# A sample delta rule with stacked single-pass outer products, and the output norm of the prompt columns dealt out over its rounds

## The chip, the core and the metric

The kernel runs on one core of a Trainium2 chip. The metric is the time on the device in microseconds (us) of the whole program, one launch. Five engines work side by side and meet only at semaphores: TensorE (PE in the profile, with PEld for its weight loads), VectorE (DVE), ScalarE (ACT), GpSimd (POOL) and SyncE (SP, which here only issues DMAs).

## What is computed

Two consecutive layers of a hybrid decoder for 256 prompt tokens and 8 sample tokens that share the weights: layer 0 is a recurrent branch beside differential attention and a dense SwiGLU; layer 1 is a gated delta rule (8 heads of 128 x 128) and a mixture of 8 experts. The change touches the delta rule's sample part and the norm of its output. For each sample b and head h the reference does one step:

```
v_new = beta * (v - exp(g) * (k . S))          # S is the 128 x 128 state of (b, h)
o     = exp(g) * (q . S) + (q . k) * v_new
S     = exp(g) * S + outer(k, v_new)            # the state is read from HBM and written back
...
o = rmsnorm(o, onorm_g) * silu(z)               # over the 128 values of each head, prompt and sample tokens alike
y = o @ w_out
```

## The kernel before

Activations lie transposed, channels on partitions and the T = 264 tokens (TP = 256 prompt columns, then TS = 8 sample columns) along the row. All float32 products of activations with weights are made in three single-pass parts: both operands are split into a float32r high part and a low rest (`h_hi`, `h_lo`, `weight_hi`, `weight_lo`), and high x high, high x low and low x high are summed in PSUM. The delta rule's own small products are plain float32 matmuls; each of them shows as two records.

Every engine has one written list of instructions in program order; nothing is scheduled. A named signal (`sig`, `at`) is a count on a semaphore, and an engine that waits for one holds back all that is behind it in its list.

After the chunked delta rule of the prompt (it ends with `S_pr`, L1552, and fills columns 0 to 255 of `oT`) comes the sample part, which is what the change rewrites. It goes through the HC = 8 heads in rounds. The states of a head (8 samples, 512 KB) lie in one of four slots of `s_ring`: heads 0 to 3 are loaded long before; the states of head h + 4 can be loaded by GpSimd's queue (L563, L744 to L746) only when those of head h have been written back by ScalarE's queue (L1138). In a round

- TensorE makes k . S and q . S of the next head (`state_products`, L2167: 8 samples, each one float32 weight load of a 128 x 128 state and 2 columns), transposes v_new and k of this head into 8 rows (`state_rows`, L2177, L2178), and makes the outer products of the head before (`state_outer`, L2186: k as an 8 x 128 weight, a block-diagonal 8 x 1024 `v_diag`, in two matmuls of 512 columns, in plain float32);
- VectorE makes v_new and o of the next head (`sample_out`, L1637 to L1642), copies the k rows and spreads v_new over the blocks of `v_diag` (`sample_outer_in`, L1650, L1651), and adds the outer products to the states (`sample_state`, L1658);
- ScalarE scales the states by exp(g) (L1132) and issues the write-back (L1138).

`v_diag` and the PSUM banks of the outer products (5, 6 and 0, 1) are double.

Behind the last round comes the output norm of all 264 columns, one engine after another: ScalarE squares (L1141), TensorE sums over each head (L2201), ScalarE takes the root (L1143), VectorE the reciprocal (L1681), TensorE spreads it over 128 partitions (L2208, 8 heads), VectorE applies it (L1684) and multiplies by the gate `zT` (L1689), ScalarE makes `h_hi` (L828) and VectorE `h_lo` (L834). TensorE then starts the projection `w_out_o` (lines L858, L862, L869), which waits for `on_hi`. Router, dispatch and the eight experts (L2287 to L2308) follow. SyncE begins to load the first expert's weights (L629) when the last states are written back, since these use the same ring.

## Time and profile before

| | us |
|---|---|
| three timed runs, median (lowest to highest) | 1877.57 (1874.33 to 1878.81) |
| the profiled execution: its own time | 1878.5 |
| the profiled execution: its span in the trace | 1876.8 |

The span runs from the first instruction to the last; 1.7 us lie around it. TensorE's matmul row is busy 1739.3 us of the span, VectorE 1357.2, ScalarE 1056.0. The granted clock is 0.928 of full speed on average. A row such as "PE bank L2186" names an engine, what it writes and the line of the kernel; a time in a chain or timeline row is counted from the start of the span.

### The profile page before, as it was taken

What the parts mean: (1) busy time and instruction counts of PE and PEld (TensorE: products, weight loads), DVE (VectorE), ACT (ScalarE), POOL (GpSimd) and SP (SyncE); (2) the same over time, 40 slices, a digit from 0 to 9 for tenths busy, and PEclk for the clock granted to TensorE, in tenths of its full rate; (3) what the DMA queues carried; (4) which work ended last, traced back from release to release, by engine and by line L of the source; (5) the groups of instructions that cost most, each with busy time, mean ns of one, the idle gap of its engine ahead of it and who ended that gap; (6) DMA issues with size and microseconds to landing.
All of it is one profiled execution on the core that took longest, in us unless ns stands there. A gap on an engine that the chain in (4) does not pass through costs nothing.

```text
span 1876.8 us, 25201 instructions
## 1 busy us (share of the span) xinstructions
PE 1739.3 (93%) x9621; PEld 1483.8 (79%) x9621; DVE 1357.2 (72%) x1519; ACT 1056.0 (56%) x1019; POOL 122.9 (7%) x149
## 2 busy tenths in 40 slices
PE   7957899999777989889999999999999999999997
PEld 7826799998766877477888888888888888888885
DVE  6673355445755783456889889888898898888986
ACT  5332344335552223236767777777677777776774
POOL 5021021003221000010000000000000000000000
PEclk9955799999987887589999999999999999999999
DMA  7542144544340001446999989989999899899893
GB/s 258 180 138 67 65 162 156 202 158 142 135 135 8 1 1 45 129 163 215 375 336 346 373 319 360 375 309 372 346 338 368 322 355 375 310 368 376 310 370 131
DMA packets 199099, 445.48 MB, mean 237 GB/s; under 512 B 9473, under 2 KB 20899, under 8 KB 198975
## 3 DMA queue, kind: packets, MB, share of 16 engines
q1 hardware_dynamic: 184698, 423.88, 62.6%
q0 software_dynamic: 3872, 12.85, 2.4%
q10 hardware_dynamic: 10448, 7.65, 1.4%
q8 instruction: 55, 0.90, 0.2%
q14 instruction: 26, 0.21, 0.0%
HBM read 437.28 MB, written 7.29 MB: 237 GB/s over the span
## 4 chain that ended last, share of the span: by engine, by line
PE 79%; DVE 9%; ACT 5%; PEld 2%; issue 2%; DMA 1%; POOL 1%; PEldq 0%; DVEq 0%; ACTq 0%; SPq 0%
PE bank L2308 16%; PE bank L2287 11%; PE bank L2288 11%; PE bank L2292 11%; PE bank L858 5%; PE bank L862 5%; PE bank L869 5%; PE bank L2258 2%; ACT weight_hi L505 1%; PE bank L2268 1%; PE bank L2186 1%; DVE weight_lo L508 1%; PE bank L2167 1%; POOL weight_lo L559 1%; PE bank L2111 1%
## 5 line engine op out<-in xcount | busy, mean ns | idle before, releaser
L508 DVE TENSOR_TENSOR weight_lo<-weight_ring,weight_hi 128x2048 fp32r<-128x2048 f32 (+1 forms) x352 | 797.0, 2273 | 258.4 <-ACT weight_hi L505 236.6
L505 ACT ACTIVATE weight_hi<-weight_ring 128x2048 fp32r<-128x2048 f32 (+1 forms) x358 | 680.0, 1903 | 335.6 <-PE bank L869 118.7
L2287 PE MATMUL bank<-weight_hi,h_lo 128*128 128x512 f32 x896 | 355.1, 396 | 4.2 <-DVE h_lo L1746 4.2
L2288 PE MATMUL bank<-weight_hi,h_hi 128*128 128x512 f32 x896 | 350.0, 391 | 0.0
L2292 PE MATMUL bank<-weight_lo,h_hi 128*128 128x512 f32 x896 | 239.9, 390 | 0.0
L2287 PEld LDWEIGHTS bank<-weight_hi,h_lo 128*128 128x128 f32 x896 | 168.8, 188 | 38.7 <-DVE h_lo L1746 4.5
L2292 PEld LDWEIGHTS bank<-weight_lo,h_hi 128*128 128x128 f32 x896 | 168.2, 188 | 35.2
L2288 PEld LDWEIGHTS bank<-weight_hi,h_hi 128*128 128x128 f32 x896 | 169.0, 189 | 33.6
L858 PE MATMUL bank<-n_hi,weight_hi 128*128 128x264 f32 x608 | 104.2, 294 | 23.3 <-ACT h_f L1072 7.9
L2308 PE MATMUL bank<-weight_hi,h_lo 128*128 128x512 f32 x448 | 120.6, 391 | 1.8 <-DVE h_lo L1751 1.8
L2308 PE MATMUL bank<-weight_lo,h_hi 128*128 128x512 f32 x448 | 119.8, 389 | 0.0
L2308 PE MATMUL bank<-weight_hi,h_hi 128*128 128x512 f32 x448 | 119.8, 389 | 0.0
L508 DVE TENSOR_TENSOR weight_lo<-work,weight_hi 128x2048 fp32r<-128x2048 f32 x48 | 109.8, 2288 | 12.6 <-ACT weight_hi L505 12.6
L858 PEld LDWEIGHTS bank<-n_hi,weight_hi 128*128 128x128 f32 x608 | 86.7, 194 | 27.6 <-issue 26.0
L505 ACT ACTIVATE weight_hi<-work 128x2048 fp32r<-128x2048 f32 x48 | 92.1, 1919 | 26.8 <-PE bank L2292 20.4
L862 PE MATMUL bank<-n_hi,weight_lo 128*128 128x264 f32 x608 | 101.5, 290 | 2.8 <-POOL weight_lo L559 2.8
L2308 PEld LDWEIGHTS bank<-weight_hi,h_lo 128*128 128x128 f32 x448 | 83.5, 188 | 18.9 <-DVE h_lo L1751 2.1
L2308 PEld LDWEIGHTS bank<-weight_hi,h_hi 128*128 128x128 f32 x448 | 84.1, 188 | 17.6
L2308 PEld LDWEIGHTS bank<-weight_lo,h_hi 128*128 128x128 f32 x448 | 84.1, 188 | 17.5
L858 PE MATMUL bank<-h_hi,weight_hi 128*128 128x264 f32 x464 | 87.9, 294 | 9.0 <-ACT h_hi L828 5.9
L862 PEld LDWEIGHTS bank<-n_hi,weight_lo 128*128 128x128 f32 x608 | 86.7, 194 | 3.2 <-POOL weight_lo L559 3.2
L862 PE MATMUL bank<-h_hi,weight_lo 128*128 128x264 f32 x464 | 85.9, 290 | 1.5 <-DVE weight_lo L508 1.5
(465 smaller groups left out, 2226.7 us busy)
## 6 DMA issues: line engine op xcount, KB each, us to landing
weight_ring<-in_moe_wg SPq DMA_DIRECT2D x104, 1024.0 KB, 7.2
weight_ring<-in_moe_wu SPq DMA_DIRECT2D x96, 1024.0 KB, 7.4
weight_ring<-in_moe_wd SPq DMA_DIRECT2D x88, 1024.0 KB, 6.6
work<-in_moe_wd SPq DMA_DIRECT2D x24, 1024.0 KB, 7.2
weight_ring<-in_w_in_o SPq DMA_DIRECT2D x8, 2048.0 KB, 8.8
work<-in_moe_wu SPq DMA_DIRECT2D x16, 1024.0 KB, 6.0
weight_ring<-in_ffn_wg SPq DMA_DIRECT2D x5, 2048.0 KB, 7.8
weight_ring<-in_ffn_wu SPq DMA_DIRECT2D x5, 2048.0 KB, 7.8
```

Of the source, the lines that this page charges most:

```text
L505: return SC.activation(whi[:, p % SPLIT, 0:size], src, ACT.Copy).then_inc(sig("hi_done"), 1)
L508: V.tensor_tensor(wlo[:, p % SPLIT, 0:size], src, whi[:, p % SPLIT, 0:size].bitcast(F32), ALU.subtract)\
L559: GP.tensor_tensor(wlo[:, p % SPLIT, 0:size], src, whi[:, p % SPLIT, 0:size].bitcast(F32), ALU.subtract)\
L858: PE.matmul(out, hi[:, jj, cols_], a_hi[:, j0 + j, :], start=first and j == 0, stop=False)
L862: PE.matmul(out, lo[:, jj, cols_], a_hi[:, j0 + part * half + jj, :], start=False, stop=False)
L869: last = PE.matmul(out, hi[:, jj, cols_], a_lo[:, j0 + j, :], start=False, stop=last_one and j == k - 1)
L2111: last = PE.matmul(bank[STREAM[u]][:, k * P:(k + 1) * P], Am[:, h, :], Tt[:, h, :], start=True, stop=True)
L2258: last = PE.matmul(bank[(7, 3)[r]][:, jj * CAP:(jj + 1) * CAP], h_tok[:, i, j * P:(j + 1) * P], sel[:, i, :], start=i == 0, stop=i == NTT - 1)
L2287: PE.matmul(out, hte_l[:, j, :], hi[:, jj, :], start=j == 0, stop=False)
L2288: PE.matmul(out, hte_h[:, j, :], hi[:, jj, :], start=False, stop=False)
L2292: last = PE.matmul(out, hte_h[:, j, :], lo[:, jj, :], start=False, stop=j == KD - 1)
L2308: last = PE.matmul(bank[5 + hf][:, :], lhs[:, c % 2, k, :], rhs[:, kk, hf * CHUNK_COLS:(hf + 1) * CHUNK_COLS], start=c == 0 and k == 0 and ...
```

## The change

It does three things, all between the end of the prompt's delta rule and the start of `w_out_o`.

1. The outer products. k and v_new are split into a float32r high part and a rest, and stacked as 24 rows: (k high, k low, k high) against (v high, v high, v low). The sum over 24 rows is the same three-part product as elsewhere, in one float32r pass of 512 columns instead of one float32 matmul. The k rows of all heads are transposed once ahead of the rounds (`k_three`, eight transposes, two ScalarE copies to `k_rows`); each round transposes only the 24 v rows. VectorE makes the v split in each round ahead of its signal (two short instructions more before `s_v`), and no longer copies k rows. `v_diag` and the outer products' banks are single instead of double, so `state_outer(h)` waits for `sample_state(h - 1)`, and `sample_outer_in(h)` for `state_outer(h - 1)`. Three small DMAs on GpSimd's queue make the 24-row selector `same_row`.
2. The norm of the 256 prompt columns is taken into the rounds: squares ahead of round 0 (ScalarE), head sums in round 0 (TensorE, behind `state_rows(0)`), root in round 1 (ScalarE), reciprocal in round 1 (VectorE, behind `sample_state(0)`), two heads' spreading and application in each of rounds 2 to 5, the gate multiplication on GpSimd (behind the loads of heads 5, 6 and 7), `h_hi` in two parts in rounds 6 and 7.
3. The norm of the 8 sample columns comes behind round 7 as one small group of its own (64 columns), with a matmul against `ones`; `sample_state(7)`, the last addition, is moved behind it. `w_out_o` waits for `on_sample_hi`.

```diff
--- before.py
+++ after.py
...
-        v_new_blocks = (inv.rearrange("p a b -> p (a b)")[:, 2 * T:2 * T + TS * P], work[:, B_0 + 4 * GRP:B_0 + 6 * GRP])
-        v_diag = [v.rearrange("p (b e) -> p b e", b=TS) for v in v_new_blocks]
...
-        k_row = [inv[0:TS, 1, k * P:(k + 1) * P] for k in range(2)]
+        R3 = 3 * TS
+        outer_in = n_lo2[:].rearrange("p a b -> p (a b)")
+        v_diag = outer_in[0:R3, HC * TS:HC * TS + TS * P].rearrange("p (b e) -> p b e", b=TS)
+        k_rows = outer_in[0:R3, HC * TS + TS * P:HC * TS + (TS + HC) * P].rearrange("p (h d) -> p h d", h=HC)
...
-        outer_banks = ((5, 6), (0, 1))
+        outer_banks = (5, 6)
...
@@ GpSimd
             gp.wait_ge(*at("tail_written", 32))
+            for k in range(3):
+                gp.dma_start(same_row[k * TS:(k + 1) * TS, :], ident[0:TS, 0:TS]).then_inc(sig("same_row_made"), 16)
             GP.memset(gt_mask, 1.0)
...
+            def gate_rows(heads_):
+                for h in heads_:
+                    gp.wait_ge(*at("on_applied", h + 1))
+                    GP.tensor_tensor(oT[:, h, 0:TP], oT[:, h, 0:TP], zT[:, h, 0:TP], ALU.mult).then_inc(sig("on_gated"), 1)
+
             for h in range(4, HC):
                 gp.wait_ge(*at(f"state{h % 4}_written", 16))
                 load_state(gp, h)
+                if h >= 5:
+                    gate_rows(range((h - 5) * 2, (h - 5) * 2 + 2))
+            gate_rows(range(6, HC))
@@ ScalarE
+            SC.activation(o_prompt_sq, oT[:, :, 0:TP], ACT.Square).then_inc(sig("on_sq"), 1)
             act_e.wait_ge(*at("s_gb", 1))
...
+            for g in range(2):
+                act_e.wait_ge(*at("s_kt", g + 1))
+                SC.activation(k_rows[:, halves[g], :], bank[(4, 7)[g]][0:R3, :].rearrange("p (h d) -> p h d", h=NG), ACT.Copy)\
+                  .then_inc(sig("s_krows"), 1)
...
             for h in range(HC + 1):
...
                     last.then_inc(sig("s_scaled"), 1)
+                if h == 1:
+                    act_e.wait_ge(*at("on_ss", 1))
+                    SC.activation(o_prompt_r, bank[0][0:HC, 0:TP], ACT.Sqrt, bias=eps_t[0:HC, :], scale=1.0 / DV).then_inc(sig("on_root"), 1)
+                if h == HC - 2:
+                    o_high(0)
+                if h == HC - 1:
+                    act_e.wait_ge(*at("s_o", HC))
+                    SC.activation(o_sample_sq, oT[:, :, TP:T], ACT.Square).then_inc(sig("on_sample_sq"), 1)
...
+                    o_high(1)
+                    act_e.wait_ge(*at("on_done", 1))
+                    SC.activation(h_hi[:, :, TP:T], oT[:, :, TP:T], ACT.Copy).then_inc(sig("on_sample_hi"), 1)
...
-            act_e.wait_ge(*at("s_o", HC))
-            SC.activation(inv, oT[:], ACT.Square).then_inc(sig("on_sq"), 1)
-            act_e.wait_ge(*at("on_ss", 1))
-            SC.activation(inv[0:HC, 0, :], bank[4][0:HC, 0:T], ACT.Sqrt, bias=eps_t[0:HC, :], scale=1.0 / DV).then_inc(sig("on_root"), 1)
-            high_parts(act_e, oT, "on_done", "on_hi")
@@ VectorE
+            link(V.tensor_copy(k_three[:, :, 0:TS].bitcast(F32R), kT[:, :, TP:T]))
+            V.tensor_copy(k_three[:, :, 2 * TS:R3].bitcast(F32R), kT[:, :, TP:T])
+            V.tensor_tensor(k_three[:, :, TS:2 * TS].bitcast(F32R), kT[:, :, TP:T], k_three[:, :, 0:TS], ALU.subtract)\
+             .then_inc(sig("s_k_three"), 1)
...
-                V.tensor_tensor(vn_t, qS, eg, ALU.mult).then_inc(sig("s_v"), 1)
+                if h >= 2:
+                    dve.wait_ge(*at("s_vt", h - 1))
+                v3 = v_three[:, h % 2, :]
+                link(V.tensor_copy(v3[:, 0:2 * TS].rearrange("p (k b) -> p k b", k=2).bitcast(F32R), vn.unsqueeze(1).broadcast_to([P, 2, TS])))
+                V.tensor_tensor(v3[:, 2 * TS:R3].bitcast(F32R), vn, v3[:, 0:TS], ALU.subtract).then_inc(sig("s_v"), 1)
+                V.tensor_tensor(vn_t, qS, eg, ALU.mult)
...
-                if h >= 2:
-                    dve.wait_ge(*at("s_outer", h - 1))
+                if h == 0:
+                    dve.wait_ge(*at("same_row_made", 48))
+                else:
+                    dve.wait_ge(*at("s_outer", h))
...
-                link(V.tensor_copy(k_row[h % 2], vt[0:TS, P:2 * P]))
-                V.tensor_tensor(v_diag[h % 2][0:TS], ident[0:TS, 0:TS].unsqueeze(2).broadcast_to([TS, TS, P]),
-                                vt[0:TS, 0:P].unsqueeze(1).broadcast_to([TS, TS, P]), ALU.mult).then_inc(sig("s_vd"), 1)
+                V.tensor_tensor(v_diag, same_row.unsqueeze(2).broadcast_to([R3, TS, P]),
+                                vt[0:R3, 0:P].unsqueeze(1).broadcast_to([R3, TS, P]), ALU.mult).then_inc(sig("s_vd"), 1)
...
+                if h == 1:
+                    dve.wait_ge(*at("on_root", 1))
+                    V.reciprocal(o_prompt_r, o_prompt_r).then_inc(sig("on_inv"), 1)
+                if 2 <= h <= 5:
+                    normed(2 * (h - 2))
+                    normed(2 * (h - 2) + 1)
...
@@ TensorE
+            pe.wait_ge(*at("s_k_three", 1))
+            for g in range(2):
+                for h in range(g * NG, (g + 1) * NG):
+                    last = PE.transpose(bank[(4, 7)[g]][0:R3, h % NG * P:(h % NG + 1) * P], k_three[:, h, :], ident[:])
+                last.then_inc(sig("s_kt"), 1)
...
-                PE.transpose(vt[0:TS, 0:P], vn_s[h % 2], ident[:])
-                PE.transpose(vt[0:TS, P:2 * P], kT[:, h, TP:T], ident[:]).then_inc(sig("s_vt"), 1)
+                PE.transpose(vt[0:R3, 0:P], v_three[:, h % 2, :], ident[:]).then_inc(sig("s_vt"), 1)
...
-                if h >= 2:
-                    pe.wait_ge(*at("s_state", h - 1))
+                if h:
+                    pe.wait_ge(*at("s_state", h))
                 for k in range(2):
                     n = TS // 2
-                    last = PE.matmul(bank[outer_banks[h % 2][k]][:, :], k_row[h % 2],
-                                     v_diag[h % 2][0:TS, k * n:(k + 1) * n, :].rearrange("p b e -> p (b e)"), start=True, stop=True)
+                    last = PE.matmul(bank[outer_banks[k]][:, :], k_rows[:, h, :],
+                                     v_diag[:, k * n:(k + 1) * n, :].rearrange("p b e -> p (b e)"), start=True, stop=True)
                 last.then_inc(sig("s_outer"), 1)
...
+                if h == 0:
+                    head_sums()
+                if 2 <= h <= 5:
+                    head_rows(2 * (h - 2))
+                    head_rows(2 * (h - 2) + 1)
...
-            pe.wait_ge(*at("on_hi", 2))
+            pe.wait_ge(*at("on_sample_hi", 1))
```

TensorE, from the last sums ahead of the rounds to the outer products of head 0; before (L2159 is the sum q . k, L2167 the state products, L2186 the outer products):

```order
L2159 MATMUL bank<-work,ones 128x64
L2167 MATMUL bank<-work,weight_ring 128x2 x16
L2177 MATMUL bank<-ident,sm 8x128
L2178 MATMUL bank<-ident,work 8x128
L2167 MATMUL bank<-work,weight_ring 128x2 x8
L2177 MATMUL bank<-ident,sm 8x128
L2178 MATMUL bank<-ident,work 8x128
L2186 MATMUL bank<-work 128x512 x2
L2167 MATMUL bank<-work,weight_ring 128x2 x8
```

and now (L2216, L2229 and L2249 are the same three; L2220 transposes the k rows, L2257 are the head sums, L2265 the spreading of the norm):

```order
L2216 MATMUL bank<-work,ones 128x64
L2220 MATMUL bank<-ident,work 24x128 x8
L2229 MATMUL bank<-work,weight_ring 128x2 x16
L2241 MATMUL bank<-ident,work 24x128
L2257 MATMUL bank<-work,sm 8x256 x8
L2229 MATMUL bank<-work,weight_ring 128x2 x8
L2241 MATMUL bank<-ident,work 24x128
L2249 MATMUL bank<-n_lo_odd 128x512 x2
L2229 MATMUL bank<-work,weight_ring 128x2 x8
L2241 MATMUL bank<-ident,work 24x128
L2249 MATMUL bank<-n_lo_odd 128x512 x2
L2265 MATMUL bank<-work,ident 128x256 x2
```

The k transposes stand in front of the first state products, the head sums between the row transposition of head 0 and the state products of head 2, and two spreading matmuls behind the outer products from round 2 on.

VectorE, from the additions of heads 5 to 7 to the start of `w_out_o` (seven short memsets stand between the first three rows and the copy); before:

```order
L1658 TENSOR_TENSOR weight_ring<-weight_ring,bank 128x512 x2
L1650 COPY work<-bank 8x128
L1651 TENSOR_TENSOR work<-ident,bank 8x1024
L1658 TENSOR_TENSOR weight_ring<-weight_ring,bank 128x512 x4
L1679 COPY work<-bank 128x128
L1681 RECIPROCAL work<-work 8x264
L1684 SCALAR_TENSOR_TENSOR hT<-hT,par,bank 128x264 x8
L1689 TENSOR_TENSOR hT<-hT,work 128x1056 x2
L834 TENSOR_TENSOR h_lo<-hT,h_hi 128x1056 x2
L508 TENSOR_TENSOR weight_lo<-weight_ring,weight_hi 128x2048
```

and now (L1695 fills `v_diag`, L1702 adds to the states, L1710 and L1737 make `h_lo`, L1732 to L1734 are the sample norm):

```order
L1695 TENSOR_TENSOR n_lo_odd<-small,bank 24x1024
L1702 TENSOR_TENSOR weight_ring<-weight_ring,bank 128x512 x2
L1695 TENSOR_TENSOR n_lo_odd<-small,bank 24x1024
L1702 TENSOR_TENSOR weight_ring<-weight_ring,bank 128x512 x2
L1710 TENSOR_TENSOR h_lo<-hT,h_hi 128x4x256
L1732 RECIPROCAL work<-work 128x64
L1733 SCALAR_TENSOR_TENSOR hT<-hT,par,work 128x8x8
L1734 TENSOR_TENSOR hT<-hT,work 128x8x8
L1710 TENSOR_TENSOR h_lo<-hT,h_hi 128x4x256
L1737 TENSOR_TENSOR h_lo<-hT,h_hi 128x8x8
L1702 TENSOR_TENSOR weight_ring<-weight_ring,bank 128x512 x2
L1740 COPY work<-bank 128x128
```

Of the norm only the 64 sample columns and the low parts are left at the end, ahead of the last addition.

GpSimd, from the last mask to the router's sums (L563 and L570 load the states of heads 4 to 7); before:

```order
L740 AFFINE_SELECT work<-work 128x8x8
L740 AFFINE_SELECT work<-work 128x4x16
L740 AFFINE_SELECT work<-work 128x2x32
L740 AFFINE_SELECT work<-work 128x64
L563 DMA weight_ring<-in_state_delta_s 128x8x128 x4
L752 TENSOR_TENSOR work<-work 128x264 x7
```

and now (L756 is the gate multiplication):

```order
L749 AFFINE_SELECT work<-work 128x64
L570 DMA weight_ring<-in_state_delta_s 128x8x128 x2
L756 TENSOR_TENSOR hT<-hT,work 128x256 x2
L570 DMA weight_ring<-in_state_delta_s 128x8x128
L756 TENSOR_TENSOR hT<-hT,work 128x256 x2
L570 DMA weight_ring<-in_state_delta_s 128x8x128
L756 TENSOR_TENSOR hT<-hT,work 128x256 x4
L769 TENSOR_TENSOR work<-work 128x264 x7
```

The loads of heads 6 and 7 now stand behind two gate multiplications each.

## Rows read from the trace of the kernel before

**Rows 1.** Windows by stage: window, length, busy us (instructions) of each engine, PEclk, DMA.

```profile
722.30:789.40 67.10, 61.98 (x182) 38.33 (x182) 28.95 (x81) 20.13 (x67) 3.56 (x4) 0.51 0.35 95
789.40:808.80 19.40, 10.45 (x33) 5.32 (x33) 10.49 (x21) 5.88 (x5) 0.00 (x0) 0.68 0.85 297
808.80:856.80 48.00, 42.87 (x327) 38.48 (x327) 21.22 (x59) 21.22 (x33) 6.73 (x7) 0.96 0.31 110
856.80:1876.80 1020.00, 1008.04 (x4712) 834.40 (x4712) 875.81 (x551) 729.26 (x497) 0.00 (x0) 1.00 0.92 337
```

**Rows 2.** The chain that ended last, in the rounds: start, length, what.

```profile
723.18 6.50 PE bank L2167 x32
...
729.92 0.21 PE bank L2178
...
733.78 3.72 PE bank L2186 x4
737.52 1.29 DVE weight_ring L1658 x2
738.84 3.22 DMA out_delta_s_sample<-weight_ring
...
742.35 4.85 DMA weight_ring<-in_state_delta_s
747.24 3.58 PE bank L2167 x16
...
780.89 7.13 PE bank L2186 x8
```

**Rows 3.** The same chain, from the last write-back to `w_out_o`.

```profile
789.78 1.97 ACT work L1141
791.80 5.29 PE bank L2201 x16
...
797.62 1.80 DVE work L1681
799.47 5.16 PE bank L2208 x16
...
805.18 2.44 DVE hT L1689 x2
...
808.78 1.25 PE bank L858 x4
```

**Rows 4.** Timeline of the rounds: VectorE's short products and its spreading of v_new.

```profile
726.41 0.17 DVE L1637 TENSOR_TENSOR sm<-bank,sm 128x8 f32<-128x8 f32 x1 [3.86 <-PE bank L2167]
...
742.30 1.21 DVE L1651 TENSOR_TENSOR work<-ident,bank 8x1024 f32<-8x1024 f32 x1
```

**Rows 5.** The chain at the experts' start: a float32r matmul of 512 columns, clock low.

```profile
857.64 0.43 PE bank L2288
```

**Rows 6.** Timeline of GpSimd: the masks, and the router's sums.

```profile
588.70 4.57 POOL L740 TENSOR_SCALAR_AFFINE_SELECT work<-work 128x64 f32<-128x64 f32 x14
...
824.91 4.01 POOL L752 TENSOR_TENSOR work<-work 128x264 f32<-128x264 f32 x3 [56.10 <-ACT work L1152]
...
835.75 0.74 POOL L752 TENSOR_TENSOR work<-work 128x264 f32<-128x264 f32 x1 [0.60 <-ACT work L1152]
```

**Rows 7.** Timeline of VectorE: the first instruction that needs the masks.

```profile
600.13 0.87 DVE L1566 TENSOR_SCALAR work<-work,sm 128x128 f32<-128x128 f32 x4 [2.87 <-ACT work L1087]
```

**Rows 8.** Windows: the granted clock (third number from the end) around the norm and `w_out_o`.

```profile
795.00:800.00 5.00, 2.61 (x12) 1.11 (x10) 1.79 (x1) 0.47 (x1) 0.00 (x0) 1.00 1.05 402
...
808.80:812.20 3.40, 3.40 (x16) 3.40 (x17) 1.22 (x2) 0.00 (x0) 0.00 (x0) 0.52 0.00 0
812.20:815.60 3.40, 3.40 (x30) 3.40 (x30) 0.00 (x0) 0.00 (x0) 0.00 (x0) 1.00 0.02 5
```

**Rows 9.** Timeline: SyncE's first expert load, and ScalarE's first split of its data.

```profile
792.64 0.92 SPq L629 DMA_DIRECT2D weight_ring<-in_moe_wg  x2
...
822.28 1.92 ACT L505 ACTIVATE weight_hi<-weight_ring 128x2048 fp32r<-128x2048 f32 x1 [3.94 <-PEq L873]
```

More of the change, by code:

```diff
@@ L103, in program @@
               ("norm2_hi", KD), ("norm2_sq", KD), ("norm2_root", 1), ("ealog", 1), ("beta", 1), ("g_absexp", 1),
[L104 to L105 removed]
+              ("l2_sq", 2), ("l2_root", 1), ("eG", 1), ("on_sq", 1), ("s_egb", 1), ("s_qks", 1), ("s_krows", 2),
+              ("on_root", 1), ("on_hi0", 1), ("on_sample_sq", 1), ("on_sample_root", 1), ("on_hi1", 1), ("on_sample_hi", 1), ("norm3_sq", KD), ("lg_row", 1), ("norm3_root", 1), ("htok", 6),
               ("xtok", 6), ("gate_exp", 1))
@@ L1658, in sample_state, with o_low, normed @@
                     last = V.tensor_tensor(s_ring[h % 4][:, k * n:(k + 1) * n, :], s_ring[h % 4][:, k * n:(k + 1) * n, :],
-                                           heads(outer_banks[h % 2][k]), ALU.add)
+                                           heads(outer_banks[k]), ALU.add)
                 last.then_inc(sig("s_state"), 1)
+            def o_low(r):
+                part = slice(r * HALF, (r + 1) * HALF)
+                dve.wait_ge(*at(f"on_hi{r}", 1))
+                V.tensor_tensor(h_lo[:, part, 0:TP], oT[:, part, 0:TP], h_hi[:, part, 0:TP].bitcast(F32), ALU.subtract).then_inc(sig(f"on_lo{r}"), 1)
+            def normed(h):
+                dve.wait_ge(*at("on_b", h + 1))
+                V.scalar_tensor_tensor(oT[:, h, 0:TP], oT[:, h, 0:TP], col("onorm_g"), bank[h % 2][:, 0:TP], ALU.mult, ALU.mult)\
+                 .then_inc(sig("on_applied"), 1)
             sample_out(0)
@@ L2196, in _ @@
                     state_outer(h - 1)
+                if h == 0:
[3 more added lines that the diff above has]
+                    head_rows(2 * (h - 2) + 1)
+            pe.wait_ge(*at("on_sample_sq", 1))
+            PE.matmul(bank[2][:, 0:HC * TS], ones[:], o_sample_sq.rearrange("p h b -> p (h b)"), start=True, stop=True)\
+              .then_inc(sig("on_sample_ss"), 1)
             state_outer(HC - 1)
             PE.matmul(bank[7][:, 0:P], ones[:], lt_mask[:], start=True, stop=True).then_inc(sig("iota_psum"), 1)
[L2199 to L2210 removed]
+            pe.wait_ge(*at("on_sample_hi", 1))
             def router_logits(tiles):
@@ L2216, in router_logits @@
                     PE.matmul(bank[3][0:NE + 1, 0:T], w_router[:, j, :], hT[:, j, :], start=j == 0, stop=False)
-            dense_pe(pe, "w_out_o", KD, "out_o_psum", "out_o_added", low=("on_lo", 2),
+            dense_pe(pe, "w_out_o", KD, "out_o_psum", "out_o_added", low=("on_sample_lo", 1),
+                     before=((5, "s_state", HC), (7, "iota", 1)),
                      between=lambda n: n and router_logits(range(HALF)))
```

67 lines of the change are left out of this document (39 added, 28 removed).

## The prediction

> **What bounds the kernel now.** First the windows by stage. The experts, 1020 us, keep TensorE busy for 1008 us at the full clock (its fourth line, [rows 1]); the change touches nothing there, so what is won before them is kept if their weights come in time. Of the 86.5 us that the change rewrites, the rounds take 67.1 and the norm behind them 19.4 [rows 1]. TensorE's 61.98 busy us in the rounds mislead: the chain of waits shows what orders them [rows 2]. TensorE makes state products (3.58 for a head at the low clock) and float32 outer products (3.72), VectorE adds (1.29), then the states are written back (738.84) and the next head's loaded into the same slot until TensorE can start on them at 747.24. So from one addition's end at 738.8 to the products 8.4 us pass in which no engine matters, and this stretch is on the chain twice (slots 0 and 3). The granted clock in the rounds is 0.51, so TensorE runs at 1.2 GHz. The norm is a chain of single engines, TensorE busy for 10.45 of 19.4 us [rows 1, 3]; nothing lies beside it.
>
> **The outer products.** A float32r matmul of 512 columns costs 0.43 at the low clock [rows 5]; two make 0.86, with the first weight load 0.95, against 3.72: 2.8 saved a head. The trace has none with 24 rows; if it cost what float32 does it would be 3.72 (upper bound), the lower bound is 0.86, and I take 0.95, since columns and type are the same as in rows 5. One of two row transpositions goes too (0.21, [rows 2]). VectorE's spreading has 1024 columns as before, 1.21 [rows 4], on 24 partitions instead of 8. Its split of v_new puts two short instructions in front of the signal, one product moves behind it: 0.2 us a round, the spacing of the 0.17 us ones [rows 4]; between nothing, where TensorE is behind anyway, and 0.4.
>
> **The entry is longer.** Three VectorE instructions and eight k transposes (0.21 each, 1.7 us) stand ahead of the first state products: 725.0 instead of 723.18, +1.8; bounds 0 and +3. The Square (1.97, [rows 3]) and the two copies of k rows on ScalarE end near 726.4, before its first scaling can start, so nothing. Then two heads' products, 7.15, one transposition 0.2, and the head sums. The old ones took 5.29 [rows 3] and now stand on the path of head 2: 5.2 taken, bounds 7.1 (low clock throughout: 7.13 / 8 = 0.89 for a float32 record of 512 columns [rows 2], half of it 16 times) and 3.6 (high throughout). Head 2's products then run 737.6 to 741.2, where they ended at 733.3 before: **+7.9 us at this point**.
>
> **The laps through the slots.** Behind head 2's products VectorE makes v_new and o (1.5), spreads (1.2) and adds (1.3): slot 0 is ready at 745.2, +6.4 against 738.8, since 3.72 is no longer in between. The root is taken by then, the reciprocal (1.75) comes behind the addition. Write and load 8.4 again [rows 2]: head 4's products 753.7 to 757.3. Then 4.0 us instead of the old 0.44 + 3.72 + 1.29 = 5.45 to the end of slot 2's addition, 761.3; load; head 6's products 769.8 to 773.3. TensorE then does transposition, outer products and two spreading matmuls (0.2 + 0.95 + 1.7) and is at 776.2, which is also when slot 3 has its states (addition 767.7 + 8.5); head 7's products end at 779.8. Before they ended at 776.2: **+3.6**. The spreading matmuls of rounds 2 to 4 and the norm's application (two a round, near 1 us on VectorE) fall into the load waits, which are 3 to 6 us long; without that cover they would cost 1.7 a round.
>
> **The end.** Single buffers make the last two heads strictly serial: v_new and o of head 7 to 781.3, spreading of head 6 to 782.5, addition 5 to 783.8, outer products 6 to 784.8, spreading 7 to 786.0, addition 6 to 787.3. Then low part of half the prompt columns 1.2, and the sample norm: reciprocal of 64 columns 0.45 (64/264 of the 1.80 of rows 3), two short products 0.5, high part 0.2: `w_out_o` starts at 789.8. My own walk of this kind gives 810.3 for the old order, where the trace has 808.78 [rows 3]; most of that excess is in the old norm, 0.3 in the rounds, so I take **789.5**. Gain 808.8 - 789.5 = **19.3 us**: the whole norm goes (19.4), the rounds' 3.6 more is given back by the shorter end. The last addition, 1.3, now runs beside `w_out_o`.
>
> **Other queues.** The three small DMAs delay GpSimd's masks by under 3 us; these end at 593.3 and are first needed at 600.1 [rows 6, 7]: nothing. The loads of heads 6 and 7 stand behind gate multiplications whose inputs are ready rounds before. The last write-back comes at 795.9 instead of 792.6 and the first expert piece is split 13.5 us behind the start of `w_out_o`, at 803 instead of 822.28 [rows 9]; the load's cover falls from 29.6 us to 7. If it is late, ScalarE waits first; TensorE needs the piece only when the experts start, 34.5 us after that split (856.8 - 822.3, [rows 1, 9]): nothing. The gate multiplication costs GpSimd 0.74 alone, but three took 4.01 [rows 6] while VectorE was subtracting from SBUF. This row is my bound: eight at up to 1.34, off the path, since the last is due only by 788.
>
> The Trainium skill, SBUF — State Buffer, section "Who interferes with whom", speaks against putting these multiplications into the rounds: a VectorE instruction with two SBUF inputs and a GpSimd one that reads SBUF exclude each other, and the second waits for the whole of the first. By that rule the 4.01 us is explained, and VectorE's short products could wait 0.7 us each in rounds 4 to 6; the sum would be 2 us higher, as the second rival has it from the rows.
>
> **The rivals.** (a) *The rounds go as walked*: 1878.5 - 19.3 = 1859.2 for the profiled execution; the median lay 0.9 below it, so 1858.3. (b) *Waits add up*: head sums wholly at the low clock (+1.9), GpSimd and VectorE holding one another up as in the 4.01 of rows 6, three times on the path (3 x 0.74 = 2.2), 0.1 more on each VectorE instruction of the chain (1.2), slower transfers with writes and loads overlapping (0.3 a leg, 1.2): up to +6, 1862 to 1867. For it: each happens singly in the rows. (c) *The clock rises in the rounds*: it went to 1.00 after 3 us of the old head sums [rows 8]. If they do the same at 735, half the sums and head 2's products gain 3, and with luck a later head too: 1851 to 1855. Against it: through eight heads of products it stayed low. (d) *The 24-row product costs what float32 does*: the walk with 3.72 starts `w_out_o` at 804.4, 1873, a gain of 5.4 that cannot be told from none. (e) *Slower: the clock stays low in* `w_out_o` *and what follows*. It began at 0.52 and stood at 1.00 in the next window [rows 8], and the 48 us stage held 42.9 us of matmuls at 0.96 [rows 1]. With TensorE doing less right before it, the rise could come later; each us later costs half a us, and if the rise never came in that stage, 40 us: 1880 to 1898. It turns into a loss once over 39 us of matmuls run low. (f) *The gain is given back to expert weights* that come late: the first split would have to come over 30 us late before it costs the first us; then 1862 to 1878.
>
> **Numbers.** (a) 0.63, (b) 0.18, (c) 0.11, (d) 0.03, (e) 0.03, (f) 0.02. The likeliest is (a), and I predict 1858.5. The range takes in (a) with 3 us on either side for the head sums and the entry, (b), and the upper part of (c): 1852 to 1866. About 0.3%, 5.6 us, is what a measurement can tell from no change. Faster by more: all of (a), (b), (c) and half of (f), 0.93; within: (d) and the rest of (f), 0.04; slower: (e), 0.03.
>
> **What would show it.** Right: outer products near 0.95 a head; head sums of about 5 us between the products of heads 1 and 2; first products at 725; TensorE still waiting for loads of heads 4 and 6; head 7's products ending near 780; `w_out_o` starting near 789.5, and 48 us from there to the experts. Wrong: outer rows of 0.9 us each; no load waits left (then VectorE or TensorE is the bound of a round); GpSimd's loads issued well after the write-back landed; ScalarE waiting for expert data near 803; a low clock past 795.

## The result, and the profile after

The changed kernel takes 1857.98 us (median of four runs, 1856.56 to 1862.84), the one before 1878.19 (1874.33 to 1879.15): a ratio of 0.9899, with a 95% interval of 0.9881 to 0.9917. The forecast was 1858.5. The profiled execution took 1856.56 us, with a span of 1854.9.

The windows by stage, with the columns of [rows 1]: rounds and sample norm, `w_out_o` to dispatch, experts.

```profile
722.30:788.50 66.20, 53.75 (x200) 39.70 (x200) 35.46 (x105) 27.09 (x77) 9.33 (x12) 0.53 0.32 88
788.50:836.60 48.10, 42.85 (x327) 38.46 (x327) 23.56 (x69) 21.19 (x33) 6.72 (x7) 0.96 0.69 241
836.60:1854.90 1018.30, 1006.73 (x4712) 833.50 (x4712) 875.46 (x552) 729.32 (x497) 0.00 (x0) 1.00 0.93 337
```

What took 86.5 us in two stages of [rows 1] is one stage of 66.2: its 20.3 us are the gain. The stage behind it is as long as before and its clock as high (48.1 and 0.96 against 48.0 and 0.96). The experts are 1.7 us shorter in this execution and 1.3 longer in another one below; the change has no part in that.

The chain that ended last, in the rounds (start, length, what), answers to [rows 2]:

```profile
723.38 1.58 PE bank L2220 x8
724.97 6.62 PE bank L2229 x32
...
731.82 6.20 PE bank L2257 x16
738.02 1.89 PE bank L2229 x16
...
742.32 1.28 DVE weight_ring L1702 x2
743.62 3.22 DMA out_delta_s_sample<-weight_ring
...
747.12 4.95 DMA weight_ring<-in_state_delta_s
...
752.12 3.57 PE bank L2229 x16
...
755.93 1.16 PE bank L2249 x2
...
758.32 1.28 DVE weight_ring L1702 x2
759.62 3.34 DMA out_delta_s_sample<-weight_ring
...
763.24 4.80 DMA weight_ring<-in_state_delta_s
...
768.08 3.57 PE bank L2229 x16
...
773.03 1.71 PE bank L2265 x4
774.74 3.56 PE bank L2229 x16
...
788.55 1.25 PE bank L875 x4
```

L2220 are the k transposes, L2229 the state products, L2257 the head sums, L1702 the additions, L2249 the outer products, L2265 the spreading matmuls, L875 the first group of `w_out_o`. The laps through slots 0 and 2 stand on the chain as forecast. TensorE's waits for the loads of the states, in total, times, longest; in the kernel before and in this one:

```profile
PE bank L2167 <- DMA weight_ring<-in_state_delta_s: 4.3, 2, 2.2
...
PE bank L2229 <- DMA weight_ring<-in_state_delta_s: 7.5, 2, 4.7
```

So the float32r products took work off TensorE, the norm's matmuls were put in, and what TensorE then still waited for loads is 7.5 us, where it was 4.3.

The profiles of this study are compared by one distance: from the prompt's last delta-rule step (720.06 in the kernel before, 720.26 in this one) to the first instruction of `w_out_o`. It is 88.7 us before and 68.3 after.

### The profile page after: what moved, and what is told of

It reads as the page before. It is cut to its first block, busy times and chain, and to the rows that moved or that the text cites. A ratio compares the mean times of both kernels' runs of the same rounds, so it can differ in the third digit from the quotient of the medians.

```text
span 1854.9 us, 25220 instructions
## 1 busy us (share of the span) xinstructions
PE 1719.8 (93%) x9607; PEld 1479.3 (80%) x9607; DVE 1354.8 (73%) x1532; ACT 1057.0 (57%) x1024; POOL 127.2 (7%) x160
## 4 chain that ended last, share of the span: by engine, by line
PE 79%; DVE 10%; ACT 4%; PEld 2%; issue 2%; DMA 1%; POOL 1%; PEldq 0%; DVEq 0%; ACTq 0%; SPq 0%
PE bank L2384 16%; PE bank L2363 11%; PE bank L2364 11%; PE bank L2368 11%; PE bank L875 5%; PE bank L879 5%; PE bank L886 5%; PE bank L2334 2%; ACT weight_hi L512 1%; PE bank L2344 1%; DVE weight_lo L515 1%; PE bank L2229 1%; POOL weight_lo L566 1%; PE bank L2168 1%; PEld bank L879 1%
## 5 line engine op out<-in xcount | busy, mean ns | idle before, releaser
L875 PE MATMUL bank<-n_hi,weight_hi 128*128 128x264 f32 x608 | 104.8, 295 | 22.9 <-ACT h_f L1089 7.9
L875 PEld LDWEIGHTS bank<-n_hi,weight_hi 128*128 128x128 f32 x608 | 87.0, 195 | 27.3 <-issue 26.0
L512 ACT ACTIVATE weight_hi<-work 128x2048 fp32r<-128x2048 f32 x48 | 92.1, 1919 | 26.8 <-PE bank L2368 20.4
L875 PE MATMUL bank<-h_hi,weight_hi 128*128 128x264 f32 x464 | 87.8, 294 | 5.3 <-DVE work L1314 1.7
```

The costliest lines, as they stand in the source:

```text
L512: return SC.activation(whi[:, p % SPLIT, 0:size], src, ACT.Copy).then_inc(sig("hi_done"), 1)
L875: PE.matmul(out, hi[:, jj, cols_], a_hi[:, j0 + j, :], start=first and j == 0, stop=False)
```

## The experiments

All kernels, one line each. The distance, the time from there to the experts' first matmul and the clock are of the profiled execution; the times and ratios are of all runs. Kernels of one set shared a chip and the runs of the kernel before, whose medians were 1879.2, 1878.4 and 1876.3 in sets 1 to 3.

| set | kernel | to `w_out_o` | to experts | mean clock | median (lowest to highest) | ratio to before (95%) |
|---|---|---|---|---|---|---|
| 0 | before | 88.7 | 48.1 | 0.928 | 1878.19 (1874.33 to 1879.15) | |
| 0 | changed | 68.3 | 48.1 | 0.932 | 1857.98 (1856.56 to 1862.84) | 0.9899 (0.9881 to 0.9917) |
| 1 | after_again | 70.0 | 48.9 | 0.930 | 1859.42 (1852.94 to 1861.37) | 0.9884 (0.9866 to 0.9903) |
| 1 | sums_late | 64.0 | 48.3 | 0.938 | 1857.08 (1849.79 to 1857.74) | 0.9885 (0.9868 to 0.9901) |
| 1 | tail_early | 63.7 | 49.9 | 0.930 | 1853.99 (1853.51 to 1856.03) | 0.9866 (0.9850 to 0.9883) |
| 1 | both | 58.8 | 50.4 | 0.937 | 1854.48 (1848.34 to 1856.04) | 0.9872 (0.9856 to 0.9889) |
| 2 | outer_only | 86.3 | 49.4 | 0.928 | 1876.15 (1868.49 to 1878.99) | 0.9988 (0.9977 to 0.9999) |
| 2 | outer_f32 | 82.3 | 47.9 | 0.927 | 1871.74 (1865.88 to 1873.34) | 0.9962 (0.9949 to 0.9976) |
| 2 | gate_dve | 67.9 | 48.1 | 0.931 | 1857.68 (1856.83 to 1860.02) | 0.9895 (0.9878 to 0.9911) |
| 2 | half_states | 64.6 | 48.2 | 0.931 | 1853.84 (1853.03 to 1856.10) | 0.9872 (0.9856 to 0.9889) |
| 3 | after_third | 64.8 | 47.9 | 0.937 | 1856.94 (1852.20 to 1858.50) | 0.9891 (0.9871 to 0.9910) |
| 3 | both_again | 62.6 | 50.4 | 0.931 | 1850.95 (1849.85 to 1854.60) | 0.9862 (0.9843 to 0.9881) |
| 3 | root_behind | 62.0 | 50.6 | 0.931 | 1851.31 (1848.96 to 1854.59) | 0.9858 (0.9837 to 0.9879) |
| 3 | rows_early | 60.2 | 49.9 | 0.931 | 1851.47 (1846.03 to 1854.23) | 0.9858 (0.9836 to 0.9880) |

### The changed kernel itself, twice more

> The changed kernel unchanged, so that the other kernels of this comparison have it beside them. Every theory: 1858 us as in its first timing (1856.6 to 1862.8), and in the trace outer products of 1.2 us a head, head sums of 6.2, the first instruction of w_out_o near 788.5.

> The changed kernel unchanged, beside the three below on one chip. Every theory: 1858 to 1860 us; where the mean granted clock of an execution is 0.938 instead of 0.931, about 6 us less, since in the earlier comparison the one such execution of it took 1852.9 and the others 1859.1 to 1861.4.

The medians lie within 1.5 us of the first, but the distance to `w_out_o` came out as 68.3, 70.0 and 64.8: 5 us between executions of one kernel. In after_again the path went through slot 1, whose write-back took 4.55 us and whose load 5.37. In after_third the clock differed. Its windows around the end of the delta rule:

```profile
600.00:720.00 120.00, 100.93 (x819) 97.38 (x818) 90.75 (x281) 32.32 (x77) 0.00 (x0) 0.91 0.01 1
715.00:720.00 5.00, 3.55 (x31) 3.20 (x30) 2.82 (x12) 1.30 (x2) 0.00 (x0) 1.00 0.04 11
720.00:725.00 5.00, 5.00 (x39) 4.93 (x37) 1.16 (x8) 4.88 (x14) 0.00 (x0) 0.77 0.33 97
```

and its chain:

```profile
720.66 4.65 PE bank L2229 x32
725.54 5.54 PE bank L2257 x16
```

The clock of the prompt's stage, which the change leaves alone, was 0.91 (0.88 in the first execution over 600 to 720), that stage ended 3.7 us earlier, and the clock fell later, so that two heads' products took 4.65 instead of 6.62 and the head sums 5.54 instead of 6.20. The three profiled executions with a mean clock of 0.937 or 0.938 (after_third, sums_late, both) all show 0.91 from 600 to 715 us and 4.65 or 4.66 for these products; the others that have the k transposes show 0.88 or 0.89 and 6.62. The one execution of after_again with a mean clock of 0.938 took 1852.9 beside 1859.1 to 1861.4. So a step of some 6 us between executions comes with the clock of a stage ahead of the change (why it differs, no run shows), and distances below are compared at like clocks.

### One part alone

outer_only: from the changed kernel, everything of the norm put back where it stood.

```
-                if h == 0:
-                    head_sums()
-                if 2 <= h <= 5:
-                    head_rows(2 * (h - 2))
-                    head_rows(2 * (h - 2) + 1)
...
+            pe.wait_ge(*at("on_sq", 1))
+            for i in range(HC):
+                last = PE.matmul(bank[4][0:HC, 0:T], pick[:, 2 * HC - 1 - i:3 * HC - 1 - i], inv[:, i, :],
...
```

> Part 1 of the change alone: stacked float32r outer products with their single buffers and the k transposes ahead of the rounds; the whole norm of 264 columns stands behind the rounds as in the kernel before. Theory (the time is won by taking the norm off the end; the outer products are on the chain only at the turns of two slots and behind the last heads): the rounds lose the 6.2 us of head sums that the changed kernel has in them, so that the last addition ends near 785.4, 4 us before the last write-back of the kernel before, the norm's chain of 19 us follows, and w_out_o starts near 804.5: a gain of 4 to 5 us, time 1873 to 1875. Rival (TensorE is the bound of the rounds, as its 61.98 busy us of 67.1 look, and 2.5 us less for each of 8 heads counts in full): w_out_o near 788, time 1858, and the norm's dealing out would be worth nothing.

A gain of 2.4 us at `w_out_o`, and 2.2 in the medians, by the interval of the ratio hardly to be told from none: the rival, by which TensorE is the bound, falls, and the theory's gain of 4 to 5 was not reached either. The rounds did what the theory said and more: TensorE waited 13.5 us for loads, where it was 4.3,

```profile
PE bank L2195 <- DMA weight_ring<-in_state_delta_s: 13.5, 4, 6.2
```

and the last addition ends 63.5 us behind the delta rule's last step, where it was 69.3, 5.7 earlier. But then the norm took 22.8 us instead of 19.5. Its chain (L2231 are the head sums, L2238 the spreading, L867 `w_out_o`), to be read beside [rows 3]:

```profile
783.53 6.35 PE bank L2231 x16
...
792.25 7.42 PE bank L2238 x16
...
803.82 1.25 PE bank L867 x4
```

and the windows:

```profile
790.00:795.00 5.00, 2.75 (x6) 2.16 (x7) 2.77 (x3) 0.37 (x1) 0.00 (x0) 0.73 1.05 387
795.00:800.00 5.00, 4.66 (x11) 2.99 (x9) 2.75 (x6) 0.00 (x0) 0.00 (x0) 0.50 0.95 350
...
805.00:810.00 5.00, 5.00 (x27) 5.00 (x26) 0.05 (x1) 0.00 (x0) 0.00 (x0) 0.57 0.00 0
```

The same matmuls that took 5.29 and 5.16 took 6.35 and 7.42, because the clock, 1.00 behind the old head sums [rows 8], was down at 0.50 during most of the spreading and 0.57 into `w_out_o`, whose stage is 1.4 us longer. Ahead of the norm TensorE now had two float32r products (1.20 each) with waits between them, where it had 7.13 us of float32 products without a gap [rows 2]. So 3.3 + 1.4 of the 5.7 us went to a lower clock. That less work ahead is the cause of the late rise fits, and was not tried by itself.

outer_f32: the other way round, the float32r pass taken back.

```
-                    last = PE.matmul(bank[outer_banks[k]][:, :], k_rows[:, h, :],
-                                     v_diag[:, k * n:(k + 1) * n, :].rearrange("p b e -> p (b e)"), start=True, stop=True)
+                    last = PE.matmul(bank[outer_banks[k]][:, :], k_rows[:, h, :].bitcast(F32),
+                                     v_diag[:, k * n:(k + 1) * n, :].rearrange("p b e -> p (b e)").bitcast(F32), start=True, stop=True)
```

> The changed kernel with one thing undone: the 24-row outer products are plain float32 matmuls, on the same rows and buffers. It measures the disputed price (24 rows in float32 against 24 rows in float32r) and what it is worth. Theory: 3.7 to 3.9 us a head instead of 1.2; since the single buffers put them in series with spreading and addition, they count at slot 0's turn, at slot 2's turn, in the rounds of heads 5 to 7 and in the end: w_out_o 15 us later, near 804, time 1873. Rival (TensorE's time in the rounds is hidden behind the loads except at the two turns): 2.6 us twice, w_out_o near 794, time 1863.

14.0 us at `w_out_o` (theory 15), 1871.7 us (theory 1873). The chain in the middle of the rounds:

```profile
756.41 3.70 PE bank L2249 x4
760.11 1.71 PE bank L2265 x4
761.82 3.50 PE bank L2229 x16
765.55 3.71 PE bank L2249 x4
769.26 1.71 PE bank L2265 x4
```

A 24-row float32 product takes 3.70 us, the old 8-row one 3.72 [rows 2]: the 16 further rows cost nothing that these rows show. No DMA stands between these rows. TensorE waited only once for a load, 1.8 us, where the changed kernel waits 7.5, so here it is the bound.

Together the two kernels say what the parts are worth. Both have the single buffers, whose own price was not measured. Stacked products alone give 2.4 us, the dealt-out norm with float32 products 6.5 (88.7 - 82.3), both 20.4. Given the other, each is worth 14 to 18: the norm needs TensorE time and free banks in the rounds, and the short products make the time. The norm dealt out over the old double buffers was not tried, since it uses banks 0 and 1, which these held.

### The lap of a slot

half_states:

```
-            gp.dma_start(s_ring[h % 4], A["state_delta_s"][0, :, h].rearrange("b d e -> d b e")).then_inc(sig(f"state{h % 4}_loaded"), 16)
+            gp.dma_start(s_ring[h % 4][:, 0:TS if h < 4 else TS // 2], A["state_delta_s"][0, 0:TS if h < 4 else TS // 2, h].rearrange("b d e -> d b e")).then_inc(sig(f"state{h % 4}_loaded"), 16)
...
-                q.dma_start(O["delta_s_sample"][0, :, h].rearrange("b d e -> d b e"), s_ring[h % 4]).then_inc(sig(f"state{h % 4}_written"), 16)
+                q.dma_start(O["delta_s_sample"][0, 0:TS // 2, h].rearrange("b d e -> d b e"), s_ring[h % 4][:, 0:TS // 2]).then_inc(sig(f"state{h % 4}_written"), 16)
```

> It leaves out samples 4 to 7 of the loads of heads 4 to 7 and of all write-backs of the states: every transfer of the rounds carries half the bytes, all computation stays. Theory (the rounds' pace is the lap write-back, issue, load of 8.4 us through slots 0 and 2): a leg shrinks by less than half, since part of it is fixed; the lap comes down to about 6.5, heads 4 and 6 have their states 1.9 us earlier each, w_out_o near 785, time about 1854. Rival 1 (the engines set the pace, the loads are hidden): w_out_o at 788.5. Rival 2 (the lap is all bytes): 4.2 us a lap, then TensorE and VectorE become the bound near 782.

Slot 0's lap in its chain:

```profile
741.84 2.32 DMA out_delta_s_sample<-weight_ring
744.44 3.60 DMA weight_ring<-in_state_delta_s
```

From addition to products 6.3 us instead of 8.5 (743.60 to 752.12 in the changed kernel), TensorE's waits for loads 3.7 instead of 7.5, `w_out_o` 3.7 earlier (theory 3.5), 1853.8 us (theory 1854; gate_dve, in the same set and within 0.4 us of the changed kernel at `w_out_o`, took 1857.7). Head 6's products began 4.8 us earlier, but head 7's then waited 1.1 us for the load of slot 3, so not all of it reached the end. Half the bytes took 72% of the write's time and 73% of the load's. If a leg is a fixed part and one that goes with the bytes, the fixed part is 1.4 us of the write's 3.22 and 2.25 of the load's 4.95 (an estimate from these rows): a little under half. Both rivals fall.

### GpSimd beside VectorE

gate_dve:

```
-                if h >= 5:
-                    gate_rows(range((h - 5) * 2, (h - 5) * 2 + 2))
-            gate_rows(range(6, HC))
...
+                dve.wait_ge(*at("on_applied", h + 1))
+                V.tensor_tensor(oT[:, h, 0:TP], oT[:, h, 0:TP], zT[:, h, 0:TP], ALU.mult).then_inc(sig("on_gated"), 1)
```

> The gate multiplication of the norm (eight of 256 columns) is made by VectorE right behind each application of the norm instead of by GpSimd. Theory: VectorE waits for TensorE in rounds 2 to 5 anyway, so 2 x 0.4 us more a round are hidden; the two short VectorE instructions that took 0.60 and 0.48 instead of 0.17 while GpSimd issued a load or multiplied come down, if GpSimd's multiplication was the reason for the second (0.48) and the issue of a load for the first (0.60, which then stays): w_out_o within 1 us of 788.5, time 1857 to 1859. Rival 1 (the two engines hold one another up on the path by more than those two rows show): 2 us faster. Rival 2 (VectorE's rounds 4 and 5 are full): 1.5 us slower.

The rows in question, in the timeline of the changed kernel:

```profile
763.24 0.92 POOL L570 DMA_DIRECT2D weight_ring<-in_state_delta_s  x1 [7.21 <-DMA out_delta_s_sample<-weight_ring]
...
763.48 0.60 DVE L1685 TENSOR_TENSOR hT<-work,sm 128x8 f32<-128x8 f32 x1
...
764.18 1.41 POOL L756 TENSOR_TENSOR hT<-hT,work 128x256 f32<-128x256 f32 x2
...
770.92 1.41 POOL L756 TENSOR_TENSOR hT<-hT,work 128x256 f32<-128x256 f32 x2
...
771.89 0.48 DVE L1676 TENSOR_TENSOR sm<-work,sm 128x8 f32<-128x8 f32 x1
```

Two VectorE instructions of 0.17 us are stretched, by 0.43 and 0.31. In gate_dve both are gone, the first too, though GpSimd still issues a load beside the same instruction (L1682 there):

```profile
760.71 0.88 POOL L570 DMA_DIRECT2D weight_ring<-in_state_delta_s  x1 [8.60 <-DMA out_delta_s_sample<-weight_ring]
...
760.98 0.17 DVE L1682 TENSOR_TENSOR hT<-work,sm 128x8 f32<-128x8 f32 x1
```

So it was the multiplication, not the issue, against what I had expected of that row. That rests on one trace: the changed kernel's records let the multiplication start at 764.18, 0.1 us behind the end of the instruction that it held up. Taking it away moved `w_out_o` by 0.4 us, less than executions differ, and the time by nothing. GpSimd's eight multiplications took 0.70 each in the rounds. The Trainium skill, SBUF — State Buffer, "Who interferes with whom": by that rule the held-up rows are explained, since both are instructions with two SBUF inputs. The trace agrees for the second, which ends just behind a multiplication (772.37 for 772.33), and gate_dve for both; the size here was 0.74 us in all.

### Where the head sums and the sample norm stand

sums_late:

```
+        rows_at = {3: (0, 1), 4: (2, 3), 5: (4, 5, 6, 7)}
...
-                if h == 0:
+                if h == 2:
                     head_sums()
-                if 2 <= h <= 5:
-                    head_rows(2 * (h - 2))
-                    head_rows(2 * (h - 2) + 1)
+                for k in rows_at.get(h, ()):
+                    head_rows(k)
```

> The head sums of the norm move from round 0 (where TensorE has work waiting behind them) to round 2, behind the outer products of head 1, where TensorE waits 4.75 us for the states of head 4; root and reciprocal follow them into round 2, and the spreading matmuls, the norm's application and the gate follow a round later (heads 0-1 in round 3, 2-3 in round 4, 4-7 in round 5). Theory (the head sums are on the path of head 2, as the prediction walked them, and the loads set the pace after that): 6.2 us leave the path ahead of head 2, but head 2's products then run at the low clock like the others (3.57 instead of 1.89), the head sums stand 1 to 2 us out of their cover of 4.75, and two spreading matmuls more fall into round 5: slot 0's addition ends near 739.5 instead of 743.6, w_out_o starts 1.9 us earlier, near 786.7; time about 1856. Rival 1 (the sums were free because the loads of heads 2 and 3 or VectorE hid them): no change, w_out_o at 788.5. Rival 2 (what counts is the clock: the sums pay for themselves by raising it for the products behind them): head 2's products at 3.57 and a sum of 7.1 at the low clock throughout take the gain back, w_out_o at 788 to 790.

At like clocks `w_out_o` is 0.8 us earlier (64.0 against 64.8), the median 2.3 lower. The theory said 1.9. Neither number can be told from none with this spread. Its timeline shows a side effect of the edit:

```profile
737.11 1.27 DVE L1703 TENSOR_TENSOR weight_ring<-weight_ring,bank 128x512 f32<-128x512 f32 x2
...
741.81 0.46 ACT L1163 ACTIVATE work<-bank,eps_t 8x256 f32<-8x256 f32 x1 [4.04 <-PE bank L2257]
741.81 0.38 ACTq L1179 DMA_DIRECT2D out_delta_s_sample<-weight_ring  x1
```

Head 1's states are ready at 738.4 and written back from 741.8, because ScalarE stands at the root, waiting for the head sums, with the write-back queued behind it.

tail_early:

```
+                if h == HC - 1:
+                    sample_norm()
                 sample_outer_in(h)
...
+            def between_out(n):
+                if n:
+                    return router_logits(range(HALF))
+                state_outer(HC - 1)
```

> Only the end of the rounds is changed: the sums of the 8 sample columns are made ahead of the outer products of head 6 instead of behind them, ScalarE's square, root and high parts and VectorE's sample norm stand ahead of the spreading of head 7, and the outer products of head 7 stand inside w_out_o, behind its first group of products. Theory (w_out_o waits for VectorE's string of spreading and additions of heads 5, 6 and 7, of which its own inputs need none): w_out_o starts 5 us earlier, near 783.5; the last addition ends near 794 instead of 790, the last states are written back 4 us later, and the first expert split comes near 806, still more than 20 us ahead of the experts: time 1853. Rival (load cover): with the write-backs and the expert loads later by the same 4 us that the start of w_out_o is earlier, the experts' weights come late, ScalarE waits in w_out_o for weights, and the gain shrinks to 0 to 2 us: w_out_o at 783.5, but the experts at 48 plus 3 to 5 us behind it.

`w_out_o` starts 4.6 us earlier than in the changed kernel (6.3 than in after_again, at the same clock), and the time is 5.4 us below after_again's: theory 5. From `w_out_o` to the experts it takes 1.7 us longer (0.9 against after_again). The rival is there, as the chain shows:

```profile
795.44 5.09 DMA weight_ring<-in_moe_wg
800.55 1.92 ACT weight_hi L512
```

In the changed kernel ScalarE's first split of expert data came 13.5 us behind the start of `w_out_o` (802.02) and waited for no load; here it is 18.6 behind (800.55 - 782.00) and waits for the load. But it cost at most the 1.7 us and not the 3 to 5 of the rival; how much of these is the outer products inside the stage and how much the load stays open.

both, and both_again (one kernel):

> The two edits before together: head sums in round 2, and the sample norm ahead of the last two heads' outer products. Theory: the gains add, since one lies ahead of slot 0's lap and the other behind the last products; w_out_o starts 5 to 7 us earlier than in the changed kernel, between 781.8 and 783.8, time 1851 to 1853. Rival (the gate multiplications and high parts of heads 4 to 7, which now come a round later, end after the sample norm would be ready): only the 5 us of the second edit, 1853, with ScalarE's high part waiting for GpSimd.

> The kernel with both edits (head sums in round 2, sample norm ahead of the last two heads' outer products) once more. Its profile had w_out_o 9.5 us earlier than in the changed kernel, counted from the last step of the prompt's delta rule, and yet its median lay only 4.9 us lower. Theory: the profiled execution was one with the higher clock (0.937), which alone makes some 6 us; at equal clock both edits give 4.5 to 5 us, 1854.5; 2 of the gain at the start of w_out_o are given back inside it, where the last outer products now stand. Rival: the edits give 9.5 us and something behind w_out_o gives 5 back.

At 0.937 the distance is 6.0 us shorter than in after_third, at 0.931 5.7 to 7.4 shorter than in the two executions near it, and 2.2 come back inside `w_out_o`: 4 to 5 net, 4.9 and 6.0 in the medians. The 9.5 us that the first profile seemed to show were a comparison across clocks. The two gains do not add as the theory had it. Against tail_early, both_again has 1.1 us less to `w_out_o` (62.6 against 63.7, at 0.931 and 0.930) and 0.5 more behind it, and in set 1 the medians of both and tail_early are 1854.5 and 1854.0. So moving the head sums is worth nothing that can be told beside the other edit. The rival's reason is not it: none of ScalarE's high parts waits for GpSimd there.

root_behind: from the kernel of both_again, the root put behind the write-back of head 1.

```
-                if h == 2:
-                    act_e.wait_ge(*at("on_ss", 1))
...
+                if h == 1:
+                    act_e.wait_ge(*at("on_ss", 1))
...
```

> Both edits, and ScalarE's root of the head sums moved from ahead of the write-back of head 1 to behind it. In the profile of the kernel with both edits ScalarE waits for the head sums to 740.7 while the states of head 1 are ready at 737.3, so their write-back starts 3.4 us late and head 5's products wait for the load to 748.8. Theory: head 5's products start 3.4 us earlier, but head 6's then wait for the load of slot 2, which is as late as before (755.3), and head 7's for the spreading matmuls of round 5: w_out_o and the time unchanged within 1 us. Rival (every lap of a slot counts): 3.4 us faster, 1851.

rows_early, from root_behind:

```
-        rows_at = {3: (0, 1), 4: (2, 3), 5: (4, 5, 6, 7)}
+        rows_at = {3: (0, 1), 4: (2, 3, 4, 5), 5: (6, 7)}
```

> The kernel before this one, and two of the four spreading matmuls of round 5 moved to round 4, where TensorE now waits for the load of head 6. Theory: in round 5 TensorE waited 2.2 us for VectorE between two pairs of spreading matmuls and then needed 2 us for the second pair, all ahead of head 7's products; without them these start 4 us earlier (with slot 3's load landing near 761.4, which root_behind brings): w_out_o 3 to 4 us earlier than in both_again, time about 1851. Rival (head 7's load then sets the time, because the transfers of slots 2 and 3 overlap): 1.5 to 2 us, 1853.

The root: 0.6 us, as expected of a wait that is not on the path. The rows: 2.4 us against both_again, where 3 to 4 were expected, so the rival was nearer. Chain of rows_early, head 1's slot:

```profile
740.93 4.96 DMA out_delta_s_sample<-weight_ring
746.18 4.56 DMA weight_ring<-in_state_delta_s
```

The write-back now runs beside head 4's load and takes 4.96 us instead of the 3.2 of one alone, which takes back part of the earlier issue: counted from the delta rule's last step it is issued 3.9 us earlier than in both_again, and head 5's products begin 2.3 earlier. In the medians both_again, root_behind and rows_early are the same, 1851.0 to 1851.5, 0.3% under the 1856.9 of the changed kernel beside them. These three beat both kernels; which of them is best was not to be told from the medians. At a like mean clock rows_early is ahead: 1850.7 to 1851.5 at 0.931 or 0.932 against 1854.3 and 1854.6 for both_again at 0.931, in few executions.

## Why the prediction was right

Times of the changed kernel are given here 0.2 us lower than in its trace, to lie in the frame of the trace before, since its delta rule took its last step 0.2 us later (720.26 for 720.06). The rows in the fences stand as they are.

- **What bounds it**: right. The laps set the pace, and half_states and outer_f32 each moved `w_out_o` by what the walk gave, 3.5 and 15 (measured 3.7 and 14.0).
- **Outer products**: 0.95 a head forecast, 1.14 to 1.21 measured. The step that failed is the reading of [rows 5]: 0.43 is the part of the chain until the next matmul, not the length of one. In the timeline at the experts' start the starts lie 0.43 apart, but each lasts 0.63:

```profile
837.69 0.63 PE L2363 MATMUL bank<-weight_hi,h_lo 128*128 128x512 f32 x1
838.12 0.63 PE L2364 MATMUL bank<-weight_hi,h_hi 128*128 128x512 f32 x1
```

  Two whose result someone waits for take 0.43 + 0.63 and the first weight load. Two of the eight pairs stand in the forecast's sum (here 1.14 at 771.89 and 1.20 at 782.33), so 0.4 us of the error reached the end; in the other rounds VectorE or a load was ready no earlier.
- **Entry**: right, 724.8 for 725.0; the copies of the k rows hid as said.
- **Head sums**: 6.20 for 5.2, inside the bounds of 3.6 and 7.1, since most ran at the low clock. Then the third rival happened in small: the clock rose under them,

```profile
735.00:740.00 5.00, 5.00 (x27) 2.77 (x25) 0.07 (x1) 0.90 (x2) 0.00 (x0) 0.78 0.00 0
740.00:745.00 5.00, 5.00 (x22) 4.25 (x21) 4.83 (x12) 0.88 (x3) 0.00 (x0) 0.56 0.09 25
```

  head 2's products ran in 1.89 instead of 3.57, and it fell again. The products of heads 0 and 1 had been put at 7.15, twice the 3.58 of a head at the low clock, though their own row in [rows 2] has 6.50; they took 6.62. So head 2's products ended at 739.7, +6.4 and not +7.9: the errors were +1.0 (head sums), -1.7 (clock), -0.5 (these products) and -0.2 (entry). VectorE's part of slot 0's turn was 0.3 shorter than the 4.0 taken.
- **Laps**: 8.5 for 8.4, both times. Head 4's products began 1.8 us earlier than forecast, head 6's 1.9, head 7's ended at 778.1 for 779.8 (+1.9 against the kernel before, for +3.6).
- **The end**: from there to `w_out_o` 10.25 for 9.7. The walk itself had given 10.0; the 0.3 taken off it for the excess of the old walk was not there, and the outer products of head 6 took 1.20 for 0.95. `w_out_o` at 788.35 for 789.5, a gain of 20.4 for 19.3.
- **Terms of nothing**: right. Gate multiplications 0.70 each, stretching VectorE by 0.74 in all, off the chain, where rival (b) had three times 0.74 on it; the selector's DMAs unseen; the first expert split at 801.8 for 803, ScalarE waiting for no load there; 48.1 us from `w_out_o` to the experts, the clock 1.00 from 795 on, so (e) did not happen here. A piece of it is what outer_only paid.
- The profiled execution came 2.6 us below the 1859.2 forecast for it: 1.1 in the rounds, the rest in the experts, where executions differ by as much (1018.2, 1021.3 and 1021.2 us in three profiles of this kernel). The errors of the sum partly cancel (in us, minus is earlier than forecast: -1.5 at head 2's products, -0.4 more by head 6's, then +0.2 and +0.6), and what is left lies under what the clock of the stage ahead moves. So the mechanism and its price were right, and a median within 0.5 us is in part luck.

## What to carry to other kernels

When a chain of single engines stands behind a loop that waits for transfers, it can be dealt out into the waits, and the waits can be made by shortening the products in the loop; neither part gave a third of what both gave. Where a wait is put into an engine's list, look what is queued behind it: a root ahead of a write-back held that up by 3.4 us, though here, off the path, moving it won only 0.6. Compare two profiles only after comparing their clocks ahead of the change.

## What the runs showed of the hardware

- Two float32 products of 512 columns cost the same with 8 rows and with 24 (3.72 and 3.70 us, granted clock 0.50); in float32r two with 24 rows took 1.14 to 1.21 at this clock, and 0.73 at 739.96 in the changed kernel, where the clock was up.
- The granted clock stood at 0.50 while TensorE's row was busy 5.00 of 5 us with state products,

```profile
725.00:730.00 5.00, 5.00 (x25) 5.00 (x25) 1.16 (x8) 2.86 (x10) 0.00 (x0) 0.50 0.07 18
```

  and rose during the head sums that followed (0.78 on average from 735 to 740). So a busy row beside a low clock is no contradiction, and the price of a product must be taken from a row at the same clock.
- A 512 KB write-back took 3.2 to 3.3 us with no load in flight, and 3.3 to 5.0 when it began beside one; half of it 2.3.
